# One step of a hybrid recurrent decoder layer: a recurrent head's ScalarE work cut into two visits, the residual input read in blocks and turned on VectorE, and three moved steps

## The chip, the cores and the metric

The kernel runs on 1 core of one Trainium2 chip. The metric is device time in microseconds (us) of one execution. TensorE (PE) does the matmuls, VectorE (DVE) and ScalarE (ACT) the elementwise work, GpSimd (POOL) one subtraction for every weight tile, and SyncE (SP) issues most of the loads. Each engine takes its instructions in the order of the program; engines wait for one another by semaphores.

## The reference

One layer for 544 rows: 512 tokens of a prompt and 32 of a sample group (8 sequences of 4). `x` is normalised, projected once, three recurrent branches are computed from the projection, each is multiplied by its part of `w_branch` and by a sigmoid gate, the sum goes through `w_out`, and a gated feed-forward with a short convolution follows.

```
proj = rmsnorm(x) @ w_in + b_in
lg   = log_sigmoid(ga @ w_gla_a2 + b_gla_a2) / 16              # decay of GLA, from 16 columns ga
o_gla = head_rmsnorm(gla(q, k, v, lg)) * g * silu(gg)
o_m   = head_rmsnorm(mlstm(...)) * g * sigmoid(mo)
log_a = 8 * sigmoid(xc @ w_r + b_r) * log_sigmoid(lambda)      # RG-LRU, a block of 128 channels is a "head" here
h     = scan(a = exp(log_a), sqrt(-expm1(2 log_a)) * sigmoid(xc @ w_i + b_i) * xc)
o_r   = h * gelu(ry)
x    += (sum_b sigmoid(G_b) * (o_b @ w_branch_b)) @ w_out
x    += (gelu(conv(u_a)) * conv(u_b)) @ w_down,   u = rmsnorm(x) @ w_up
y     = rmsnorm(x)
```

The outputs are `y` and the new states of all recurrences. All arrays are f32. The kernel gets close to f32 by splitting each operand into a high and a low part and making three matmul passes (high·high, high·low, low·high).

## The kernel before, in words

Activations lie with channels on partitions and the 544 rows along the free dimension. The work is a list of **units**, one for each tile of 128 output columns. A unit of `w_in`, `w_out` or `w_up` has 8 tiles of K, so 8 x 3 passes x 2 halves of 272 rows = 48 matmuls. Units 0 to 28 are the projection (0: small columns, among them `ga`; 1 to 8: q, k, v; 9 to 12: mLSTM's input; 13 to 16 and 17 to 20: RG-LRU's `rx` and `ry`; 21 to 24: `gg`; 25 to 28: `mo`). Units 29 to 52 ("gate and branch") have 48 matmuls for a gate and, after a slot in which other work may stand, 24 for the branch. 29 to 36 use GLA's output, 37 to 44 RG-LRU's, 45 to 52 mLSTM's. Units 53 to 60 are `w_out`, 61 to 104 `w_up`, then `w_down`.

A unit's weights go the same way each time: SP loads them into one of two `stage` slots (`free_stage` waits until POOL is done with the unit two before), ACT rounds them to `whi` (`hi`, L1122 and L1131; it also waits until the matmuls of the unit two before are done), POOL makes `wlo = stage - whi` (`lo`, L523), PE runs the matmuls (L602), and ACT takes the result out of PSUM (`evac`). PE may begin unit u when `lo` of u is there and `evac` of u-2 is done, so it needs `evac` of 25 for unit 27, and `evac` of 28 for unit 29.

The recurrent work runs between units. A table, filled by `plan(unit, part, steps)`, says which steps each of PE, ACT, DVE and POOL makes at each unit (part 0: after the unit; part 1: in the slot between gate and branch). All engines walk the same table, each doing its share of a step, and in the order in which the steps were planned. ACT at a unit does `hi` of u+2, `evac` of u, and then its steps.

The steps that the change and the prediction touch:

- `a2`: PE multiplies `ga` by `w_gla_a2` (L689); ACT takes two Abs out of PSUM (L1228) and goes on with Exp and Ln; DVE adds up the decays (`bc`).
- `rg` i: the gates of RG-LRU head i, 8 matmuls on PE (L808), then on ACT two Sigmoid, Tanh, Exp and Sqrt (L1329 to L1338), each kind of function with a table load of its own.
- `rgd` i: DVE's part of the same head (L1928 to L1946), with the scan L1938; L1942 ends what ACT waits for before the next head (`rg_o`), L1946 signals `or`. L1931 needs ACT's Sqrt.
- `gfin`: DVE's last step on GLA's output (L1904, L1907, L1909), which signals `og`. ACT waits for `og` before its `evac` of unit 25 (L1219).
- `rh`: PE transposes the last states of RG-LRU, in unit 31's slot; it waits for the fourth `or`.
- `sH` h, `sI` h: the state update of mLSTM for the samples. The states pass through three buffers; head 3 uses buffer 0 again, and its load waits until buffer 0 has been stored (`ch_out`).
- The residual `x`: it is loaded again as rows (`xp2`, `xs2`, after unit 48's load), and between units 53 and 54 PE turns it with 40 transposes (L591) into PSUM, from which DVE copies it to `xt` (L2126). DVE then clears `fraw` and `ssa`; SP waits for `ssa`, loads `fraw` (L463) and only then the weights of unit 57. DVE adds unit 53 to `xt` (L2136), which PE needs before unit 55.

Of the kernel before, what the change touches and what calls it, by code (L numbers as in the profile page):

```python
# [88 lines left out]
def layer(nc, io):  # L89
    ctx = ExitStack()  # L90
    with ctx:
# [270 lines left out]
        def _(sp):  # L362
# [70 lines left out]

            for n in range(3):
# [5 lines left out]
                def pair_of_units(i):  # L440
                    for r in range(2):
                        slot = (u0 + r) % 2
                        free_stage(i * 2 + (u0 + r))
                        load(slot, one(gates, i * 2 + r), KT_IN)
                        sp.dma_start(stage[:, slot, KT_IN:KT_GB], one(outs, i * 2 + r)).then_inc(s(f"branch{slot}"), 16)

                done = 0
                if n == 2:
                    done = 2
                    for i in range(done):  # L450
                        pair_of_units(i)

                    sp.wait_ge(s("om"), 1)
# [1872 lines left out]
```

## Time and profile before

| | us |
|---|---|
| median of 3 runs (lowest, highest) | 991.7 (988.83, 995.17) |
| the profiled execution | 993.07 |
| its span in the trace | 991.3 |
| busy: PE | 969.4 (98%) |
| busy: DVE, ACT, POOL | 539.4, 402.8, 310.8 |

The profile is of one execution. The span is from its first to its last instruction; the execution's own time is 1.8 us longer. A busy PE says that a matmul was in flight, not that it ran at full clock: the granted clock is a column of its own, 1.00 for 2.4 GHz and 0.50 for 1.2 GHz. With PE busy for 98% of the span, time can come or go only where PE is idle, where its clock is down, or where it does less or more.

### The profile page before, as it was taken

To read this page: it belongs to the slowest core of one execution; us is meant where nothing else is said; L and a number is where in the kernel's file an instruction comes from. 1 tells how busy PE (TensorE), PEld (TensorE's weight loads), DVE (VectorE), ACT (ScalarE), POOL (GpSimd) and SP (SyncE) were. 2 spreads that over 40 slices of the span, in tenths; PEclk is the share of its full clock that TensorE was granted. 3 is DMA by queue.
4 is the path that set the end of the run, shared out by engine and by line. 5 is a ranking of instruction groups with operands and counts; after the bars stand their busy time and mean duration, and the time that the engine had idled before them with its cause. 6 is when DMAs were issued, how large, how long until landed. Compare 5 with 4: busy or idle time off the path is not lost.

```text
span 991.3 us, 19378 instructions
## 1 busy us (share of the span) xinstructions
PE 969.4 (98%) x7550; PEld 948.7 (96%) x7550; DVE 539.4 (54%) x906; ACT 402.8 (41%) x584; POOL 310.8 (31%) x301
## 2 busy tenths in 40 slices
PE   9999999999799999899999999999999999999997
PEld 8899999898799999899999999999999999999996
DVE  5586346677725357764225467776777777312122
ACT  5632433477525555123232344444444444222122
POOL 2653433245322234333543530010000000244440
PEclk9999999999999999999999999999999999999998
DMA  5235423244122223526224422333222223533222
GB/s 149 65 86 117 108 65 81 64 111 128 47 72 64 65 64 87 159 63 209 73 65 61 103 85 85 89 94 93 85 85 85 85 85 101 122 93 88 87 59 91
DMA packets 172018, 89.62 MB, mean 90 GB/s; under 512 B 13662, under 2 KB 169956, under 8 KB 171967
## 3 DMA queue, kind: packets, MB, share of 16 engines
q1 hardware_dynamic: 154341, 79.16, 29.0%
q10 hardware_dynamic: 17626, 9.74, 3.8%
q8 instruction: 37, 0.61, 0.2%
q14 instruction: 14, 0.11, 0.0%
HBM read 82.29 MB, written 6.32 MB: 89 GB/s over the span
## 4 chain that ended last, share of the span: by engine, by line
PE 44%; issue 35%; POOL 18%; ACT 1%; DMA 1%; POOLq 0%; DVE 0%; DVEq 0%
PE ps L602 42%; POOL wlo L523 18%; PE ps L1040 1%; PE ps L591 1%; DMA xtok<-x_prompt 1%; PE ps L661 0%; ACT junk L1144 0%; PE ps L627 0%; POOLq L557 0%; PE ps L620 0%; ACT xtok L1160 0%; PE ps L1031 0%; PE ps L1032 0%; ACT whi L1122 0%; POOL blkc L513 0%
## 5 line engine op out<-in xcount | busy, mean ns | idle before, releaser
L523 POOL TENSOR_TENSOR wlo<-stage,whi 128x384 fp32r<-128x384 f32 (+3 forms) x231 | 278.3, 1232 | 428.2 <-ACT whi L1122 332.7
L602 PE MATMUL ps<-xh,whi 128*128 128x272 f32 x1536 | 322.6, 291 | 4.0 <-POOL wlo L523 3.4
L602 PE MATMUL ps<-xh,wlo 128*128 128x272 f32 x1536 | 318.6, 289 | 0.0
L602 PE MATMUL ps<-xl,whi 128*128 128x272 f32 x1536 | 317.7, 288 | 0.0
L602 PEld LDWEIGHTS ps<-xh,whi 128*128 128x128 f32 x1536 | 242.8, 189 | 9.1 <-ACT qk L1201 2.5
L602 PEld LDWEIGHTS ps<-xl,whi 128*128 128x128 f32 x1536 | 242.0, 189 | 0.0
L602 PEld LDWEIGHTS ps<-xh,wlo 128*128 128x128 f32 x1536 | 240.5, 189 | 0.0
L1122 ACT ACTIVATE whi<-stage 128x1024 fp32r<-128x1024 f32 (+3 forms) x59 | 72.1, 1222 | 148.3 <-PE ps L602 131.2
L1131 ACT ACTIVATE whi<-stage 128x1024 fp32r<-128x1024 f32 (+1 forms) x54 | 59.9, 1109 | 147.3 <-PE ps L602 142.0
L575 POOL COPY up<-fst 128x16 f32 (+1 forms) x44 | 25.7, 586 | 227.9 <-DVE ca L2182 227.1
L2182 DVE SCALAR_TENSOR_TENSOR ca<-up,par,ca 128x560 f32<-128x560 f32 x88 | 70.3, 799 | 6.1 <-DVE ca L2182 3.2
L602 PE MATMUL ps<-hh,whi 128*128 128x272 f32 x330 | 69.0, 291 | 0.0
L602 PE MATMUL ps<-hl,whi 128*128 128x272 f32 x330 | 68.2, 287 | 0.0
L602 PE MATMUL ps<-hh,wlo 128*128 128x272 f32 x330 | 68.1, 288 | 0.0
L2172 DVE TENSOR_TENSOR wlo<-stage,whi 128x1024 fp32r<-128x1024 f32 (+1 forms) x44 | 54.7, 1243 | 10.0 <-ACT whi L1131 6.0
L2222 DVE TENSOR_TENSOR yb<-xt,ps 128x544 f32<-128x544 f32 x7 | 5.0, 721 | 87.3 <-PE ps L602 87.3
L602 PEld LDWEIGHTS ps<-hl,whi 128*128 128x128 f32 x330 | 52.1, 188 | 0.0
L602 PEld LDWEIGHTS ps<-hh,whi 128*128 128x128 f32 x330 | 51.5, 188 | 0.1
L602 PEld LDWEIGHTS ps<-hh,wlo 128*128 128x128 f32 x330 | 51.6, 188 | 0.0
L1464 ACT ACTIVATE sg<-ps,par 128x544 f32<-128x544 f32 x24 | 17.1, 714 | 80.3 <-PE ps L602 74.4
L2162 DVE TENSOR_TENSOR up<-ps,rstd 128x272 f32<-128x272 f32 x44 | 19.4, 442 | 53.0 <-PE ps L602 53.0
L2106 DVE TENSOR_TENSOR sg<-sg,ps 128x544 f32<-128x544 f32 x16 | 11.5, 719 | 59.1 <-PE ps L602 56.5
(440 smaller groups left out, 1350.7 us busy)
## 6 DMA issues: line engine op xcount, KB each, us to landing
stage<-w_in SPq DMA_DIRECT2D x52, 512.0 KB, 3.9
stage<-w_up SPq DMA_DIRECT2D x44, 512.0 KB, 3.7
stage<-w_down SPq DMA_DIRECT2D x16, 704.0 KB, 4.4
stage<-w_branch SPq DMA_DIRECT2D x24, 256.0 KB, 4.2
...
```

The lines of the kernel that those rows point to most:

```text
L523: ins = pool.tensor_tensor(wlo[:, slot, a:b, 0:n], stage[:, slot, a:b, 0:n], whi[:, slot, a:b, 0:n].bitcast(F32), ALU.subtract)
L575: pool.tensor_copy(fsam(row[:, FPW:PADF])[:, :, 0:FW - 1], fs).then_inc(s("pads"), 1)
L591: return nc.tensor.transpose(out, in_, ident[0:k, 0:k])
L602: ins = mm(dst[:, r, :], w[:, slot, k0 + k, :], x(k)[:, r * HT:(r + 1) * HT], start=first and k == 0 and q == 0, stop=last and k == n - 1 ...
L1040: ins = mm(halves(1)[:, r, :], w[:, slot, k, :], x[:, KT_DOWN + k, r * HT:(r + 1) * HT], start=False, stop=k == KT_DOWN - 1 and q == 2)
L1122: func(whi[:, slot, 0:kt, 0:n], stage[:, slot, 0:kt, 0:n], ACT.Copy).then_inc(s("hi"), 1)
L1131: func(whi[:, slot, 0:kt], stage[:, slot, 0:kt], ACT.Copy).then_inc(s("hi"), 1)
L1464: func(split(sg[:]), halves(0), ACT.Sigmoid, bias=col).then_inc(s("gate_ev"), 1)
L2106: v.tensor_tensor(split(sg[:]), split(sg[:]), halves(1), ALU.mult).then_inc(s("br_mul"), 1)
L2162: v.tensor_tensor(row[:, FW - 1:FW - 1 + HT], src[:, 0, :], rstd[:, 0:HT], ALU.mult)
L2172: v.tensor_tensor(wlo[:, slot, 0:kt], stage[:, slot, 0:kt], whi[:, slot, 0:kt].bitcast(F32), ALU.subtract)\
L2182: v.scalar_tensor_tensor(out=out, in0=row[:, t:t + CONVF], scalar=par[:, bass.ds(j + (P_FW + 2 * NF * t + NF * r), 1)], in1=out, op0=ALU.m ...
```

## The change

Five parts. (1) `a2` moves into the middle of unit 1 on PE, and ACT's two Abs stand before `hi` of unit 3. (2) The residual `x` is loaded in blocks of 32 x 32 elements (36 DMAs, spread behind the loads of units 49 to 54) into `xq`, DVE turns it with 8 block transposes, and PE's 40 transposes go. (3) SP no longer waits for the stored mLSTM states before that load. (4) ACT issues the load of mLSTM head 3's state in `sI` 1 and not in `sH` 1. (5) ACT's chain of each RG-LRU head is cut: `rg` (Sigmoid, Sigmoid, Tanh) after units 23, 25, 27, 29, `rge` (Exp, Sqrt) a unit later; PE's and DVE's part of a head stand with `rg`. The diff shows, in this order, the table, SP's loads, PE (unit 1, then the transposes that go), ACT (the head's second half, `sI`, the loop over the units) and DVE.

```diff
+        for i in range(4):
+            plan(23 + 2 * i, 0, ("rg", i), ("rgd", i))
+            plan(*((24 + 2 * i, 0) if i < 3 else (30, 1)), ("rge", i))
         plan(24, 0, ("gfin", 0))
-        for i in range(3):
-            plan(24 + 2 * i, 0, ("rg", i), ("rgd", i))
-        plan(30, 1, ("rg", 3))
-        plan(30, 0, ("rgd", 3))
...
+            def tokens_in(k):
+                for a in range(4):
+                    part = io["x_prompt"][0].rearrange("(j t) (k a f) -> k a t j f", t=32, a=4, f=32)[k, a]
+                    dst = xq[32 * a:32 * a + 32, k, 0:SEQ].rearrange("p (j f) -> p j f", f=32)
+                    sp.dma_start(dst, part).then_inc(s("late_in"), 16)
+                if k < 4:
+                    part = io["x_sample"].rearrange("b t (k a f) -> a (b t) k f", a=4, f=32)[k]
+                    sp.dma_start(xq[32 * k:32 * k + 32, :, SEQ:T], part).then_inc(s("late_in"), 16)
...
-                    sp.wait_ge(s("ch_out"), 64)
-                    sp.dma_start(xp2[:], io["x_prompt"][0].rearrange("(t p) d -> p t d", p=P)).then_inc(s("late_in"), 16)
-                    sp.dma_start(xs2[:], io["x_sample"].rearrange("b t d -> (b t) d")).then_inc(s("late_in"), 16)
+            for q in range(4):
+                unit_in(2 + q // 2, q % 2)
+                tokens_in(q)
+            for q in range(2):
+                free_stage(U_OUT + q)
+                load((U_OUT + q) % 2, one(tiles(w_out, 0, KD), q), KT_IN)
+                tokens_in(4 + 2 * q)
+                tokens_in(5 + 2 * q)
...
+                if u == 1:
+                    pe.wait_ge(s("lo"), 2)
+                    gemm(halves(1), 1, 0, 4, x_of(xh), x_of(xl), last=False)
+                    v_a2(0)
+                    gemm(halves(1), 1, 4, 4, x_of(xh, 4), x_of(xl, 4), first=False).then_inc(s("gemm"), 1)
+                    continue
...
-            for j in range(KD):
-                if j >= 2:
-                    pe.wait_ge(s("xt"), j - 1)
-                for t in range(4):
-                    tr(pair(2 + j % 2)[:, t * P:(t + 1) * P], xp2[:, t, j * P:(j + 1) * P], P)
-                tr(pair(2 + j % 2)[:, SEQ:T], xs2[:, j * P:(j + 1) * P], TS).then_inc(s("xt_tr"), 1)
...
+            def v_rge(i):
                 act.wait_ge(s("rg_t"), 2 * i + 1)
                 func(rt[2][:, 0:CONVM], rt[2][:, 0:CONVM], ACT.Exp, scale=c8[:, i:i + 1]).then_inc(s("rg_t"), 1)
                 func(rt[4][:, 0:CONVM], rt[4][:, 0:CONVM], ACT.Sqrt).then_inc(s("rg_u"), 1)
...
             def v_sI(h):
                 if h == H - 1:
                     rms_of(NMC, TS)
+                if h == 1:
+                    act.wait_ge(s("ch_out"), 16)
+                    act.dma_start(ch_buf[0][:], io["state_mlstm_C"][0].rearrange("b h v k -> h v b k")[3])\
+                       .then_inc(s("ch_in3"), 16)
...
             for u in range(U_GB):
+                if u == 1:
+                    a2_abs()
                 act.wait_ge(s("gemm"), u + 1)
...
+            dve.wait_ge(s("late_in"), 576)
             for j in range(KD):
-                dve.wait_ge(s("xt_tr"), j + 1)
-                v.tensor_copy(xt[:, j, :], pair(2 + j % 2)[:, 0:T]).then_inc(s("xt"), 1)
+                v.transpose(xt[:, j, :], xq[:, j, :]).then_inc(s("xt"), 1)
+            dve.wait_ge(s("xt"), KD)
```

DVE, after the mLSTM convolution, at units 23 and 24. Before, `gfin` (`gv`, `ogh`, `ogl`) stands first and then head 0:

```order
L1904 SCALAR_TENSOR_TENSOR gv<-gv,par,gg 128x544 [waits s_t3_copied,s_evac]
L1904 SCALAR_TENSOR_TENSOR gv<-gv,par,gg 128x544 x3
L1907 CAST ogh<-gv 128x2176 [waits s_dve_step]
L1909 TENSOR_TENSOR ogl<-gv,ogh 128x2176 [waits s_stored,s_dve_step]
L1928 TENSOR_TENSOR rt_118<-rt_118,rx 128x568 [waits s_rg_copied]
L1931 SCALAR_TENSOR_TENSOR rt_119<-rt_117,rt_119 128x568 [waits s_rg_u,s_rg_t]
L1932 TENSOR_TENSOR rt_119<-rt_119,rt_118 128x568 [waits s_dve_step]
```

The same place on DVE in the changed kernel:

```order
L1942 TENSOR_TENSOR rt_117<-rt_117,rx 128x568 [waits s_rg_copied]
L1945 SCALAR_TENSOR_TENSOR rt_118<-rt_116,rt_118 128x568 [waits s_rg_u,s_rg_t]
L1946 TENSOR_TENSOR rt_118<-rt_118,rt_117 128x568 [waits s_dve_step]
...
L1960 TENSOR_TENSOR orl<-rt_119,orh 128x544 [waits s_dve_step]
L1918 SCALAR_TENSOR_TENSOR gv<-gv,par,gg 128x544 [waits s_t3_copied,s_evac]
L1918 SCALAR_TENSOR_TENSOR gv<-gv,par,gg 128x544 x3
L1921 CAST ogh<-gv 128x2176 [waits s_dve_step]
L1923 TENSOR_TENSOR ogl<-gv,ogh 128x2176 [waits s_stored,s_dve_step]
```

All of head 0 now stands ahead of `gfin`, the head's wait for ACT's Sqrt (`s_rg_u`) included.

ACT at units 24 and 25 before (the first row is `hi` of unit 26, `gg` is `evac` of 24, `mo` is `evac` of 25):

```order
L1122 ACTIVATE whi<-stage 128x1024 [waits s_gemm,s_stage0]
L1213 ACTIVATE gg<-ps,par 128x544 [waits s_gemm]
L1109 DMA s_gla_S<-ss 64x8x128 [waits s_out,s_ss_new]
L1109 DMA s_gla_S<-ss 64x8x128 x3
L1329 ACT_TABLE_LOAD [waits s_mcv]
L1329 ACTIVATE rt_117<-ps,par 128x568 [waits s_rg_mm]
...
L1338 ACTIVATE rt_119<-rt_119 128x568
L1122 ACTIVATE whi<-stage 128x1024 [waits s_gemm,s_stage1]
L1219 ACT_TABLE_LOAD [waits s_ss_new,s_og]
L1219 ACTIVATE mo<-ps,par 128x544 [waits s_gemm]
```

ACT from unit 23's steps on in the changed kernel:

```order
L1340 ACT_TABLE_LOAD [waits s_mcv]
L1340 ACTIVATE rt_116<-ps,par 128x568 [waits s_rg_mm]
L1341 ACTIVATE rt_117<-ps,par 128x568
L1346 ACTIVATE rt_118<-rt_116,sml 128x568 [waits s_c4,s_rg_copied]
L1131 ACTIVATE whi<-stage 128x1024 [waits s_gemm,s_stage0]
L1222 ACT_TABLE_LOAD
L1222 ACTIVATE gg<-ps,par 128x544 [waits s_gemm]
L1350 ACT_TABLE_LOAD
L1350 ACTIVATE rt_116<-rt_116,sml 128x568 [waits s_rg_t]
...
L1228 ACT_TABLE_LOAD [waits s_ss_new,s_og]
L1228 ACTIVATE mo<-ps,par 128x544 [waits s_gemm]
```

A head's first half now stands before `hi` of 26, its second half behind `evac` of 24; `evac` of 25 still waits for `s_og`.

DVE where the residual is turned, in the changed kernel:

```order
L2140 STREAM_TRANSPOSE xt<-xq 128x544 [waits s_late_in,s_stored]
L2140 STREAM_TRANSPOSE xt<-xq 128x544 x7
L2142 MEMSET up 128x2x2 [waits s_xt]
L2143 MEMSET fraw 128x1408
L2144 MEMSET ssa 128x544
L2151 TENSOR_TENSOR xt<-xt,ps 128x544 [waits s_gemm]
```

Before, eight copies from PSUM stood in place of the transposes, each behind five of PE's.

## Rows read from the trace of the kernel before

**Rows 1.** The page: busy us, share of the span, instructions of each engine.

```profile
PE 969.4 (98%) x7550; PEld 948.7 (96%) x7550; DVE 539.4 (54%) x906; ACT 402.8 (41%) x584; POOL 310.8 (31%) x301
```

**Rows 2.** Waits of PE: engine, line, awaited, us in total, times, longest.

```profile
PE ps L591 <- DVE orl L1946: 5.5, 1, 5.5
PE ps L602 <- POOL wlo L523: 3.8, 5, 2.0
PE ps L911 <- ACT cts L1418: 2.5, 1, 2.5
```

**Rows 3.** Windows: stretch, us, busy time of the engines, PE's granted clock, DMA.

```profile
272.00:277.00 5.00, 5.00 (x26) 4.78 (x26) 0.00 (x0) 0.59 (x1) 0.00 (x0) 0.57 0.47 133
```

**Rows 4.** Timeline of ACT, units 23 to 25: start, us, instruction, [idle before].

```profile
208.64 1.04 ACT L1122 ACTIVATE whi<-stage 128x1024 fp32r<-128x1024 f32 x1
...
212.24 1.28 ACT L1329 ACT_TABLE_LOAD   x1 [1.95 <-issue]
...
215.72 1.28 ACT L1337 ACT_TABLE_LOAD   x1
...
219.10 0.68 ACT L1338 ACTIVATE rt<-rt 128x568 f32<-128x568 f32 x1
...
222.04 0.71 ACT L1219 ACTIVATE mo<-ps,par 128x544 f32<-128x544 f32 x1
```

**Rows 5.** Timeline of DVE, `gfin` and head 0.

```profile
210.32 4.39 DVE L1904 SCALAR_TENSOR_TENSOR gv<-gv,par,gg 128x544 f32<-128x544 f32 x4 [4.97 <-ACT gg L1213]
...
216.07 2.43 DVE L1909 TENSOR_TENSOR ogl<-gv,ogh 128x2176 fp32r<-128x2176 f32 x1
...
219.89 0.75 DVE L1931 SCALAR_TENSOR_TENSOR rt<-rt,rt 128x568 f32<-128x568 f32 x1 [0.73 <-ACT rt L1338]
...
225.50 0.72 DVE L1942 TENSOR_TENSOR rt<-rt,ry 128x32 f32<-128x32 f32 x1
...
227.48 1.41 DVE L1946 TENSOR_TENSOR orl<-rt,orh 128x544 fp32r<-128x544 f32 x1
```

**Rows 6.** Timeline of PE: start of unit 27, and `rh` in unit 31.

```profile
225.10 0.49 PE L602 MATMUL ps<-xh,whi 128*128 128x272 f32 x2 [1.12 <-POOL wlo L523]
...
271.90 1.02 PE L591 MATMUL ps<-ident,rhn 128*9 128x128 f32 x4 [5.53 <-DVE orl L1946]
```

**Rows 7.** Timelines of PE and ACT around `a2`, and PE's start of unit 4.

```profile
33.26 2.10 PE L689 MATMUL ps<-ga,wa 16*128 16x272 f32 x8
35.39 1.32 ACT L1228 ACTIVATE g<-ps,par 128x544 f32<-128x544 f32 x2 [0.15 <-PE ps L689]
49.54 0.49 PE L602 MATMUL ps<-xh,whi 128*128 128x272 f32 x2 [1.96 <-POOL wlo L523]
```

**Rows 8.** Timeline of PE: the same 16 matmuls of `sI` for heads 1 and 2.

```profile
409.99 3.33 PE L911 MATMUL ps<-cts,qbm 128*32 128x129 f32 x16 [2.53 <-ACT cts L1418]
...
424.49 1.96 PE L911 MATMUL ps<-cts,qbm 128*32 128x129 f32 x16
```

**Rows 9.** Timeline of PE: its first transposes of `x`, and the starts of units 54 and 57.

```profile
529.51 0.60 PE L591 MATMUL ps<-ident,xp 128*128 128x128 f32 x4
...
535.98 0.52 PE L602 MATMUL ps<-mh,whi 128*128 128x272 f32 x2
...
554.75 0.52 PE L602 MATMUL ps<-mh,whi 128*128 128x272 f32 x2 [0.41 <-POOL wlo L523]
```

**Rows 10.** Timeline of DVE: the last `ml`, and `ssa` cleared.

```profile
526.17 1.32 DVE L2120 TENSOR_TENSOR ml<-mix,mh  x1 [0.83 <-ACT mh L1491]
...
538.36 0.51 DVE L2129 MEMSET ssa<- 128x544 f32 x1
```

**Rows 11.** Timeline of SP's `fraw` loads, and of ACT's `hi` of unit 57.

```profile
538.90 2.71 SPq L463 DMA_DIRECT2D fraw<-state_ffn_conv  x4
...
549.91 1.06 ACT L1131 ACTIVATE whi<-stage 128x1024 fp32r<-128x1024 f32 x1 [5.34 <-DMA stage<-w_out]
```

**Rows 12.** The line of DVE's block transpose: duration ns min/median/max, start, form.

```profile
L2153 DVE STREAM_TRANSPOSE fst<-fraw x1: 1630/1630/1630, 583.0 to 583.0; 128x1408 f32<-128x1408 f32 x1
```

More of the change, by code:

```diff
@@ L438, in _, with unit_in @@
                 u0 = U_GB + KD * n
-                def pair_of_units(i):
-                    for r in range(2):
[L442 to L453, printed above, removed]
-                    sp.wait_ge(s("ch_out"), 64)
-                    sp.dma_start(xp2[:], io["x_prompt"][0].rearrange("(t p) d -> p t d", p=P)).then_inc(s("late_in"), 16)
-                    sp.dma_start(xs2[:], io["x_sample"].rearrange("b t d -> (b t) d")).then_inc(s("late_in"), 16)
-                with sp.Fori(done, KD // 2) as i:
-                    pair_of_units(i)
-            load_all(U_OUT, tiles(w_out, 0, KD), 4, KT_IN)
+                def unit_in(i, r):
+                    slot = (u0 + r) % 2
+                    free_stage(i * 2 + (u0 + r))
+                    load(slot, one(gates, i * 2 + r), KT_IN)
+                    sp.dma_start(stage[:, slot, KT_IN:KT_GB], one(outs, i * 2 + r)).then_inc(s(f"branch{slot}"), 16)
+                with sp.Fori(0, KD // 2 if n < 2 else 2) as i:
+                    for r in range(2):
+                        unit_in(i, r)
+            sp.wait_ge(s("om"), 1)
+            for q in range(4):
[6 more added lines that the diff above has]
+                tokens_in(5 + 2 * q)
+            load_all(U_OUT + 2, tiles(w_out, 2 * P, KD - 2), 2, KT_IN)
             sp.wait_ge(s("ssa"), 1)
@@ L927, in nothing @@
                 pass
-            parts = {"a2": v_a2, "csn": nothing, "decays": nothing, "rgc": nothing, "rowc": nothing, "mconv": nothing, "rgd": nothing, "rows": nothing, "rowst": nothing, "smp": nothing, "rowt": v_rows, "gprep": nothing, "gA": v_gA, "gB": v_gB, "gd": v_gd, "gfin": nothing,
+            parts = {"a2": v_a2, "csn": nothing, "decays": nothing, "rgc": nothing, "rowc": nothing, "mconv": nothing, "rge": nothing, "rgd": nothing, "rows": nothing, "rowst": nothing, "smp": nothing, "rowt": v_rows, "gprep": nothing, "gA": v_gA, "gB": v_gB, "gd": v_gd, "gfin": nothing,
                      "cs": v_cs, "rg": v_rg, "rh": v_rh, "gelu": nothing, "mprep": nothing, "msilu": nothing, "mqk": v_mqk, "mA": v_mA, "mB": v_mB,
@@ L949, in _ @@
             for u in range(1, U_GB):
-                if u >= 2:
-                    pe.wait_ge(s("evac"), u - 1)
+                if u == 1:
[4 more added lines that the diff above has]
+                    continue
+                pe.wait_ge(s("evac"), u - 1)
                 unit(u, u % 2, u % 2, xh, xl)
@@ L1222, in _, with a2_abs @@
             a2v = ps[:, 2048:4096].rearrange("p (j a b) -> p j a b", j=2, a=2)[:, :, :, 0:HT]
[L1224 removed]
+            def a2_abs():
                 act.wait_ge(s("a2"), 1)
@@ L1228, in v_a2 @@
                     func(split(g1[:, j, :]), a2v[:, j], ACT.Abs, bias=par[:, P_A2 + j:P_A2 + j + 1]).then_inc(s("a2_act"), 1)
+            def v_a2(_):
                 act.wait_ge(s("a2_act"), 2)
@@ L1444, in nothing @@
                 pass
-            parts = {"a2": v_a2, "csn": nothing, "decays": v_decays, "rgc": nothing, "rowc": nothing, "mconv": nothing, "rgd": nothing, "rows": nothing, "rowst": v_rowst, "smp": nothing, "rowt": v_rows, "gprep": v_gprep, "gA": v_gA, "gB": v_gB, "gd": nothing, "gfin": v_gfin,
+            parts = {"a2": v_a2, "csn": nothing, "decays": v_decays, "rgc": nothing, "rowc": nothing, "mconv": nothing, "rge": v_rge, "rgd": nothing, "rows": nothing, "rowst": v_rowst, "smp": nothing, "rowt": v_rows, "gprep": v_gprep, "gA": v_gA, "gB": v_gB, "gd": nothing, "gfin": v_gfin,
                      "cs": v_cs, "rg": v_rg, "rh": v_rh, "gelu": v_gelu, "mprep": v_mprep, "msilu": v_msilu, "mqk": v_mqk, "mA": v_mA, "mB": v_mB,
@@ L2248, in _ @@
             output(1, 1, U_DOWN + 3)
-            dve.wait_ge(s("late_in"), 112)
+            dve.wait_ge(s("late_in"), 656)
             gained(0, 0, 0)
```

13 lines of the change are left out of this document (3 added, 10 removed).

## The prediction, made before the changed kernel was run

> **What bounds the kernel now.** I read the page's first part, then PE's waits, then windows and timelines around each wait. PE is busy 98% of the span [rows 1], so nothing is gained by a faster helper unless it ends an idle stretch of PE. There are three with a name [rows 2]: 5.5 us before `rh`, where DVE ends RG-LRU's fourth head late; 2.5 us in `sI` of mLSTM head 1, where ACT held back `cts`; and 3.8 us in five pieces before units that lacked `wlo`, of which 1.96 are before unit 4 [rows 7] and 0.41 before unit 57 [rows 9]. An idle stretch also costs behind its end. After the 5.5 us PE's granted clock averages 0.57 over 5 us [rows 3], so part of them was at 1.2 GHz instead of 2.4: 5 x 0.43 = 2.2 us lost. After the 2.5 us the same 16 matmuls took 3.33 us instead of 1.96 [rows 8]: 1.4 lost. The change also takes PE's transposes away, which occupy PE from 529.51 to 535.98, 6.5 us [rows 9]. Added up, 5.5 + 2.2 + 2.5 + 1.4 + 6.5 = 18.1 us are on offer. Whether they are got depends on what is late next.
>
> **Part 1, the heads and `og` (the largest term).** The order of the steps on DVE decides. Before, DVE does `gfin` from 210.32 to 218.50 [rows 5], while ACT goes through head 0's functions, 212.24 to 219.78 [rows 4]: side by side. Now `gfin` stands behind head 0 on DVE, and head 0 stands behind ACT's Sqrt, which is a unit later in ACT's order. ACT's `evac` of 25 waits for `og`, and PE's unit 27 for that `evac`. Step by step, in the times of the trace:
>
> - ACT ends mLSTM's last activation at about 208.7 (`hi` of 26 follows at 208.64 [rows 4]) and now starts the head there. Table load, two Sigmoid and Tanh take 215.72 - 212.24 = 3.5, to 212.2. `hi` of 26 takes 1.0, `evac` of 24 with a table load 1.3 + 0.7: 215.2. Exp and Sqrt with a load each take 219.78 - 215.72 = 4.1: 219.3.
> - DVE's head 0 from L1931 to the end of L1946 takes 228.89 - 219.89 = 9.0 [rows 5], part of it beside POOL's `lo`; I take 8.5: 227.8. `gfin` took 8.2; its cast and subtraction (1.3 + 2.4) and four operations at about 0.75 each give 6.7 as the low end. I take the low end, since POOL has nothing to do by then: `og` at 234.5, between 234 and 237.
> - ACT's table load and `mo` take 2.0 [rows 4]: 236.5. PE starts unit 27 at 236.7 instead of 225.10 [rows 6]. That is 11.6 us later, after some 13 us of idleness (it has done what is ahead of unit 27 by 223.7).
>
> The rest keeps ACT and DVE on the path. From 236.5: Sigmoid and Tanh of head 1, now without a table load, 2.2; `hi` 1.0; `evac` 0.7; Exp and Sqrt 4.1: 244.5. DVE gets from L1931 to the end of L1942 in 226.22 - 219.89 = 6.3: 250.8. ACT's first half of head 2 takes 2.2, `hi` of 30 1.5, `evac` of 28 0.7: 255.2. Unit 29 needs that `evac`; PE has been done since 250.8, so it idles 4.5 us. Exp and Sqrt follow to 259.3. PE makes unit 29 in 9.1 (72 matmuls at the 6.14 us for 48 of [rows 9], less a rounding) and head 3's matmuls in 1.8: 266.3. ACT's first half ends at 268.7, unit 30's gate at 272.4, its Sigmoid at 273.2, Exp and Sqrt at 277.3, DVE's head 3 at 277.3 + 8.1 to 9.0 = 285.4 to 286.3. PE has been waiting for it in `rh` since 281.6. So the wait that this part was to end is still there, 4 us long, and `rh` starts at about 285.8 instead of 271.90 [rows 6]: **+13.9 us**. The clock after the first idle stretch is hidden (PE waits for ACT again at unit 29); after the second it is not, and delays the gates that ACT waits for: +1.7, between the 1.4 of [rows 8] and the 2.2 of [rows 3]. After `rh` it costs what it did, or 0.5 less. Sum **+15** (12 to 18).
>
> **Part 2, `a2`.** PE's 2.0 us of `a2` [rows 7] move from behind unit 1 to its middle, so unit 1 ends 2.0 later, with up to 0.3 for the parameters that DVE is still copying. ACT's path from the end of unit 1 to unit 4's weights loses the two Abs and their wait, 0.15 + 1.35 = 1.5 [rows 7], since they are done in the idle time ahead. The rest of the path (`hi`, `evac`, Exp, Ln, `hi` of 4, `lo`) is as long as before. 2.0 + 0.2 - 1.5 = **+0.7** at unit 4, whose idle time grows from 1.96 to about 2.5. Nothing is behind it that was waiting.
>
> **Part 3, the load in `sI` 1.** ACT's `cts` copy stood behind the wait for the stored buffer. Without it the copy can follow PE's transposes of the states at once, which end three us before PE reaches `sI` at 409.99 - 2.53 = 407.46. Both the idle time and the clock loss go: 2.53 + 1.37 = **-3.9** [rows 8]. The load is issued about a microsecond later than before and needed some 20 us on.
>
> **Part 4, the residual.** PE runs unit 54 at 529.5 at once. DVE starts after the last `ml` at 527.5 [rows 10]. Its block transpose of 1408 columns took 1.63 us [rows 12]; 544 columns at the same rate are 0.63, with a fixed part 0.67, so eight are 5.4 (the low end; 6.5 if each costs 0.8 beside POOL's `lo`, which falls into this time). Clearing takes 2.2 as before, so `ssa` is clear at about 535.1 to 536.2 instead of 538.87 [rows 10]. The gain is that, not PE's 6.5: SP issues the four `fraw` loads only after `ssa` and the weights of unit 57 behind them, and those were already late [rows 11]. From `ssa` to the start of unit 57 it took 554.75 - 538.87 = 15.9 us, through these DMAs, `hi` and `lo`, and it still will, so unit 57 starts 2.7 to 3.8 us earlier, I take 3.5. PE, which has 12.9 us of work from unit 55 on in that time, idles 3 us before 57 (0.41 before), and pays a clock loss like part 3's, 1.4. Together **-2.1** (-3.8 to 0).
>
> This term rests on the blocks being there by 527.5. They are 36 loads of 32 KB and 64 KB in pieces of 128 bytes, as `fraw`'s are; SP issued four of 88 KB in 2.7 us [rows 11]. 2.1 MB at `fraw`'s rate (0.35 MB while 538.9 to about 546) are 40 us of the 60 us between the loads of units 49 and 56, beside the weights' 2 to 3 us each of six or so. It fits with some 3 us left at the end. The Trainium skill (DMA: Bandwidth & Descriptors, Specifications) says that below 512 bytes a transfer does not reach line rate; `fraw`'s rate agrees, and by that rule the last blocks are the ones at risk, which is the rival below. The waits dropped on SP (part 3 of the change's list) were over when SP came to them: no gain.
>
> **Sum.** +15.0 + 0.7 - 3.9 - 2.1 = +9.7. Against the profiled execution's 993.07 that is 1002.8; the median of the runs lies 1.4 lower, and from it the sum is 1001.4. I say 1002.
>
> **The rivals.**
> 1. *The wait for `og` does not reach PE, and the kernel gets faster.* If `og` came by 222, when PE is done with unit 26, part 1 would be -5.5 - 2.2 = -7.7 and the sum -13: 979. For it speaks that each half of a head fits into ACT's time between two units (3.5 and 4.1 of 6.1). Against it, that DVE needs 8.5 + 6.7 us after a Sqrt that ends at 219.3; the turning point is 12 us away. Between the two, a shorter `og` delay lets the later idle times shrink only one for one.
> 2. *The blocks land late.* If 128-byte pieces cost half as much again as `fraw`'s, the last ones land at about 531 to 532 and unit 55's weights behind them. DVE starts 4 us later, part 4 turns to +2: sum +14, 1006. For: six DMAs' weights share the queue, and unit 57's load behind `fraw` took 7.8 us to 549.8 where others took 3.5 to 4. Against: nothing else is on the queues there.
> 3. *The stretch in part 1 is shorter than I sum it*: PE's clock stays up, DVE without POOL beside it takes the low end each time. Part 1 is +12, part 4 the full -3.8: sum +5, 997.
> 4. *ACT's longer order loses more*: a late `hi` behind a long chain makes POOL late as well, with the 1 to 2 us that DVE's operations lose beside POOL: part 1 is +18, sum +13 to +16, up to 1008. The Trainium skill (SBUF — State Buffer, SBUF: two separate sides) says that a VectorE operation with two SBUF inputs and a GpSimd one shut each other out for a whole instruction. By it `gfin`, whose operations have two inputs, would be back at its 8.2 us if a `lo` fell into it, +1.5 for part 1; the low value that I took for it needs POOL idle.
>
> **How the numbers follow.** The main case, 0.60: 999 to 1005, likeliest 1002. Rival 1: 0.06. Rival 2: 0.10. Rival 3: 0.14. Rival 4: 0.10. For 8 in 10 the range takes the main case, rival 3 and most of rivals 2 and 4, and leaves rival 1 out: 995 to 1008. One per cent, 9.9 us, is what a measurement of this kernel can tell from no change, and 1001.6 lies in the middle of the main case: slower by over 1%: half of it and a little more (0.34), rivals 2 and 4 (0.19), together 0.53. Faster by over 1%: 0.06. Within 1%: 0.41.
>
> **What would show it.** In the profile after: PE's longest wait before unit 27, on ACT's `mo`, 11 to 15 us; ACT waiting for DVE's `ogl` there; a second of 4 to 5 us before unit 29, and still one of 3 to 5 us in `rh` on `orl`; the clock at 0.5 behind each. No wait on `cts`. Unit 4's wait at 2.4 to 2.8. No L591 on `xp`, eight STREAM_TRANSPOSE of 0.6 to 0.8 from about 13 us later in the span, DVE not waiting for a DMA before them, and a wait of 2 to 3.5 us before unit 57 on `wlo`. Wrong would be: unit 27 without a wait of over 5 us, or DVE waiting on `xq`'s loads.

## The result and the profile after

| | before | changed | ratio, 95% interval |
|---|---|---|---|
| median of 15 runs each (lowest, highest) | 990.2 (988.74, 995.17) us | 996.65 (995.59, 998.03) us | 1.0062 [1.0052, 1.0071] |
| the profiled execution: own time, span | 993.07, 991.3 us | 997.2, 995.4 us | |

The changed kernel is 6.4 us slower, 0.6%. That is inside the forecast range (995 to 1008), 5 us below its value, and within 1% of no change; the forecast had given the larger chance to over 1%.

The page of the changed kernel, first part (busy us, share, instructions):

```profile
PE 964.6 (97%) x7510; PEld 946.9 (95%) x7510; DVE 532.5 (53%) x906; ACT 404.0 (41%) x585; POOL 308.6 (31%) x301
```

PE has 40 instructions and 4.8 us of work fewer than in [rows 1], and the time is longer: what was saved in work came back as waiting. The waits of PE, to be held against [rows 2]:

```profile
PE ps L612 <- ACT mo L1228: 13.5, 2, 11.2
PE ps L612 <- POOL wlo L533: 4.1, 3, 2.4
PE ps L601 <- DVE orl L1960: 4.1, 1, 4.1
```

The wait on `cts` is gone, the one in `rh` has only shrunk from 5.5 to 4.1, and there are 13.5 us of a new kind: PE waits for ACT's `mo`, the `evac` of a unit. The timeline of PE at those places (start, us, instruction, [idle before]): units 4, 27 and 29, `rh`, the 16 matmuls of `sI` for heads 1 and 2, and unit 57.

```profile
50.15 0.49 PE L612 MATMUL ps<-xh,whi 128*128 128x272 f32 x2 [2.43 <-POOL wlo L533]
...
234.11 0.82 PE L612 MATMUL ps<-xh,whi 128*128 128x272 f32 x2 [11.22 <-ACT mo L1228]
...
253.11 0.55 PE L612 MATMUL ps<-xh,whi 128*128 128x272 f32 x2 [2.26 <-ACT mo L1228]
...
285.01 1.02 PE L601 MATMUL ps<-ident,rhn 128*9 128x128 f32 x4 [4.12 <-DVE orl L1960]
...
421.02 1.96 PE L921 MATMUL ps<-cts,qbm 128*32 128x129 f32 x16
...
434.14 1.96 PE L921 MATMUL ps<-cts,qbm 128*32 128x129 f32 x16
...
558.92 0.52 PE L612 MATMUL ps<-mh,whi 128*128 128x272 f32 x2 [1.54 <-POOL wlo L533]
```

Set each start against the same one of before, and the differences give the balance sheet of the two profiled executions. PE is done with unit 26 at 234.11 - 11.22 = 222.89, before at 225.10 - 1.12 = 223.98 [rows 6]: 1.1 us *ahead*, although unit 4 began 0.6 later [rows 7]. Unit 27 then starts 9.0 late and `rh` 13.1 late [rows 6]; PE comes to `sI` 1 13.6 late (421.02 for 409.99 - 2.53, since it no longer waits there) and to `sI` 2 9.65 late [rows 8]; unit 57 is 4.2 late [rows 9], the end of the span 4.1.

The clock explains the 1.1 us ahead. Windows of the changed kernel and, last, of before (stretch, us, busy time of PE, PEld, DVE, ACT, POOL, granted clock, DMA share, GB/s):

```profile
226.00:239.00 13.00, 4.89 (x21) 4.89 (x22) 6.67 (x7) 6.88 (x9) 1.86 (x3) 0.51 0.13 40
...
284.00:291.00 7.00, 5.99 (x27) 5.75 (x28) 1.55 (x3) 2.46 (x3) 0.00 (x0) 0.51 0.46 119
...
558.00:564.00 6.00, 5.08 (x40) 5.08 (x41) 3.67 (x4) 1.78 (x3) 3.99 (x4) 1.00 0.36 107
...
45.00:60.00 15.00, 12.57 (x101) 12.38 (x100) 13.99 (x31) 7.71 (x10) 9.82 (x9) 1.00 0.26 72
```

```profile
45.00:60.00 15.00, 13.04 (x92) 12.86 (x91) 13.00 (x30) 7.10 (x9) 8.64 (x8) 0.89 0.26 72
```

PE ran at 1.2 GHz (0.51) behind the waits before unit 27 and in `rh`, and at 2.4 GHz (1.00) behind those before units 4 and 57. Behind the wait before unit 29 it was at 1.2 GHz for 3.4 us as well, 1.7 us lost. Before, the stretch around unit 4 averaged 0.89: 15 x 0.11 = 1.7 us lost, which the changed kernel did not lose in this execution.

Where the 11.2 us come from. ACT of the changed kernel (Sqrt of head 0, then the table load and `mo` of unit 25), and DVE (head 0 from Sqrt on, its last operation, `gfin`):

```profile
217.57 0.68 ACT L1351 ACTIVATE rt<-rt 128x568 f32<-128x568 f32 x1
218.16 1.04 ACT L1131 ACTIVATE whi<-stage 128x1024 fp32r<-128x1024 f32 x1
232.05 1.28 ACT L1228 ACT_TABLE_LOAD   x1 [12.85 <-issue]
233.35 0.71 ACT L1228 ACTIVATE mo<-ps,par 128x544 f32<-128x544 f32 x1
```

```profile
218.36 0.75 DVE L1945 SCALAR_TENSOR_TENSOR rt<-rt,rt 128x568 f32<-128x568 f32 x1 [7.18 <-ACT rt L1351]
...
224.69 0.73 DVE L1960 TENSOR_TENSOR orl<-rt,orh 128x544 fp32r<-128x544 f32 x1
225.33 2.87 DVE L1918 SCALAR_TENSOR_TENSOR gv<-gv,par,gg 128x544 f32<-128x544 f32 x4
...
229.56 2.43 DVE L1923 TENSOR_TENSOR ogl<-gv,ogh 128x2176 fp32r<-128x2176 f32 x1
```

DVE sits idle for 7.18 us for ACT's Sqrt, does head 0 in 7.0 and `gfin` in 6.7, and at 232.0 gives `og`. The label `<-issue` on ACT's 12.85 us names no releaser; `ogl`'s end at 231.99 with the table load at 232.05 does.

### The profile page after: what moved, and what is told of

It is laid out like the page before. It is cut to its first block, busy times and chain, and to the rows that moved or that the text cites. A ratio compares the mean times of both kernels' runs of the same rounds, so it can differ in the third digit from the quotient of the medians.

```text
span 995.4 us, 19319 instructions
## 1 busy us (share of the span) xinstructions
PE 964.6 (97%) x7510; PEld 946.9 (95%) x7510; DVE 532.5 (53%) x906; ACT 404.0 (41%) x585; POOL 308.6 (31%) x301
## 4 chain that ended last, share of the span: by engine, by line
PE 45%; issue 35%; POOL 18%; POOLq 0%; ACT 0%; DVE 0%; DVEq 0%
PE ps L612 42%; POOL wlo L533 18%; PE ps L630 1%; PE ps L1049 1%; PE ps L601 1%; PE ps L637 0%; PE ps L671 0%; POOLq L567 0%; PE ps L1040 0%; PE ps L1041 0%; ACT whi L1131 0%; POOL blkc L523 0%; PE ps L1009 0%; POOLq L528 0%; DVE ytok L2285 0%
## 5 line engine op out<-in xcount | busy, mean ns | idle before, releaser
L612 PE MATMUL ps<-xh,whi 128*128 128x272 f32 x1536 | 323.9, 292 | 16.1 <-ACT mo L1228 13.5
```

The costliest lines, as they stand in the source:

```text
L612: ins = mm(dst[:, r, :], w[:, slot, k0 + k, :], x(k)[:, r * HT:(r + 1) * HT], start=first and k == 0 and q == 0, stop=last and k == n - 1 ...
```

## The experiments

All of them are held against runs of the kernel before on the same chip. "Ratio" is to those. The first four rows are from one chip, the next four from a second, the last four from a third. The kernel before itself spreads over 6.6 us, so a difference between two rows can come out up to 2 us apart by the medians and by the ratios (0.001 of ratio is 1 us); where that matters both are given.

| kernel | median us | ratio, 95% interval |
|---|---|---|
| gfin_first | 992.03 | 1.0007 [0.9993, 1.0021] |
| gfin_first_head3_whole | 985.69 | 0.9941 [0.9919, 0.9963] |
| heads_whole | 984.52 | 0.9923 [0.9894, 0.9952] |
| before_cut_only | 1003.12 | 1.0121 [1.0095, 1.0148] |
| two_sets | 979.09 | 0.9876 [0.9853, 0.9898] |
| heads_whole_a2_behind | 982.42 | 0.9914 [0.9898, 0.9931] |
| heads_whole_rh_late | 983.67 | 0.9936 [0.9915, 0.9956] |
| heads_whole_head3_early | 975.99 | 0.9849 [0.9829, 0.9870] |
| head3_early_a2_behind | 976.50 | 0.9857 [0.9831, 0.9883] |
| unit57_ahead_of_fraw | 974.97 | 0.9836 [0.9810, 0.9863] |
| before_load_in_sI | 988.07 | 0.9970 [0.9954, 0.9986] |
| before_residual_only | 985.76 | 0.9949 [0.9933, 0.9966] |

**gfin_first.** The theory taken from the prediction: the place of `gfin` behind head 0 makes the loss.

```diff
-        for i in range(4):
+        plan(23, 0, ("rg", 0))
+        plan(24, 0, ("gfin", 0), ("rge", 0), ("rgd", 0))
+        for i in range(1, 4):
             plan(23 + 2 * i, 0, ("rg", i), ("rgd", i))
             plan(*((24 + 2 * i, 0) if i < 3 else (30, 1)), ("rge", i))
-        plan(24, 0, ("gfin", 0))
```

> The changed kernel with one edit to the table: DVE does gfin before head 0 instead of behind it (head 0's rgd is planned at unit 24 behind gfin; ACT keeps the cut). Theory A (the order of DVE's steps): the 11.2 us before unit 27 and the 2.3 us before unit 29 exist only because og stands behind head 0. Then og is ready by about 218, unit 27 starts at about 223 without a wait, and the heads run two units apart; head 3's Exp and Sqrt still stand in unit 30's slot, so DVE ends it at about 268.5 and PE, there at 265, waits some 3 us in rh. Against the changed kernel that is -14 to -16.5 us: 980 to 983 us. Rival B (the cut itself: hi and evac between the halves make every head later on ACT, and PE waits for evac of 27 or for weights instead): PE waits 5 us or more before one of units 26 to 29 though og is early, and the time stays at 990 or more.

Measured 992.0: 4.6 below the changed kernel, not 14 to 16.5. Theory A fell, as far as it said "only"; the time is rival B's. PE's waits, then ACT at the first halves of heads 1 and 2 and the `evac` of unit 28, then the end of `gfin` on DVE:

```profile
PE ps L613 <- ACT mo L1229: 6.9, 1, 6.9
PE ps L613 <- POOL wlo L534: 6.3, 5, 2.4
PE ps L602 <- DVE orl L1961: 4.1, 1, 4.1
```

```profile
229.89 0.73 ACT L1341 ACTIVATE rt<-ps,par 128x568 f32<-128x568 f32 x1 [4.71 <-DVE rt L1957]
...
244.79 0.73 ACT L1341 ACTIVATE rt<-ps,par 128x568 f32<-128x568 f32 x1 [3.70 <-DVE rt L1957]
...
248.23 0.69 ACT L1229 ACTIVATE mo<-ps,par 128x544 f32<-128x544 f32 x1
```

```profile
220.69 2.43 DVE L1924 TENSOR_TENSOR ogl<-gv,ogh 128x2176 fp32r<-128x2176 f32 x1
```

`og` is there at 223.1 and the 11.2 us before unit 27 are gone (2.15 are left, on `wlo`), and 6.9 stand before unit 29. ACT comes to a head's first half and finds DVE not through with the head ahead (4.71 and 3.70 us), because both heads use the same temporaries. `hi` and `evac` stand behind that on ACT. So there were two mechanisms one behind the other, and the first had covered the second. The new theory (C): the cut brings the first half of head i to ACT one unit earlier, but the event that it needs, DVE's end of head i-1, comes no earlier.

**gfin_first_head3_whole.** `rge` 3 planned at (29, 0) instead of in unit 30's slot:

```diff
-            plan(*((24 + 2 * i, 0) if i < 3 else (30, 1)), ("rge", i))
+            plan(24 + 2 * i if i < 3 else 29, 0, ("rge", i))
```

> As gfin_first, and head 3's second half (Exp, Sqrt) is planned directly behind its first, after unit 29, so that head 3 is not cut. Theory A: Sqrt of head 3 ends at about 256 instead of 260.4, DVE ends the head at about 264, before PE is there (265): no wait in rh and no lower clock behind it. 3 us of waiting and 1.5 to 2 us of clock below gfin_first: 975 to 978 us. Rival B': ACT's 4 us of Exp and Sqrt ahead of unit 30's gate make that gate late and PE waits before unit 30's branch or unit 31 instead; then the time equals gfin_first's within 1 us.

The level was wrong with gfin_first's; the step was right and larger than forecast: 6.3 us below gfin_first, no wait in `rh` and no lower clock there. Of the 6.3, 4.1 are the wait. gfin_first's clock was at 0.50 for 6.8 us around `rh`, 5.6 of them behind PE's start there, so 2.8 us were lost; 0.6 comes back as waiting before unit 57. Rival B' fell.

**two_sets** tests theory C by taking away what ACT waits for.

```diff
+        rtb = [rt[0], rt[1], at("rt6", [P, PADM], rest + 4 * TB - 2304)]
+        def heads_rt(i):
+            return rt[:2] + (rtb if i % 2 else rt[2:5]) + [rt[5]]
...
-                if i:
-                    act.wait_ge(s("rg_o"), i)
+                rt = heads_rt(i)
+                if i > 1:
+                    act.wait_ge(s("rg_o"), i - 1)
```

> As gfin_first_head3_whole (985.7 us; PE waits 2.2 before unit 27, 0.9 before unit 28, 6.9 before unit 29), and heads 1 and 3 use a second set of three temporaries, so that ACT's first half of head i waits for DVE's head i-2 and no longer for head i-1. gfin_first overturned the theory that only the place of gfin counts: og came by 223 and unit 27 began at 226.8, but unit 29 still waited for mo, whose evac stands on ACT behind the first half of head 2, and that stood 3.7 us behind DVE's head 1. Theory C (the cut brings each head's first half to ACT a unit earlier, while DVE's end of the head ahead stays where it was, so ACT stands there with hi and evac behind it): without that wait ACT runs through, the 6.9 us before unit 29 fall to under 1, and with them 3.4 us of lower clock: 975 to 978 us. Rival D (the heads' work on ACT is simply too long for the time between the units, with two more table loads a head): ACT is behind even without the wait, unit 29 still waits 4 us or more: 982 to 986 us.

979.1 us, 1.1 above theory C's range, 2.9 below rival D's. PE's waits, and ACT's `hi` of unit 30:

```profile
PE ps L616 <- POOL wlo L537: 6.4, 5, 2.4
PE ps L616 <- ACT mo L1232: 2.3, 1, 2.3
```

```profile
242.75 1.48 ACT L1135 ACTIVATE whi<-stage 128x1536 fp32r<-128x1536 f32 x1 [2.37 <-PE ps L616]
```

The wait before unit 29 fell from 6.9 to 2.3, and the lower clock behind it is gone. The second set pays 6.6 us (6.4 by the ratios): C holds for most of it. The 2.3 us left (2.26, the figure of the changed kernel too) were not foreseen, and are no head's: ACT is through with its half of head 2 and stands idle for 2.37 us until PE ends unit 28. In the kernel before, PE's eight matmuls of head 2 stood between units 28 and 29 and covered ACT's `hi` and `evac` of 28 (the wait was 0.34); the new table has them before unit 28, so `hi` (1.5) and `evac` (0.7) lie open.

**heads_whole** undoes the cut in the changed kernel; **before_cut_only** makes the cut alone in the kernel before.

```diff
+        plan(24, 0, ("gfin", 0))
+        for i in range(3):
+            plan(24 + 2 * i, 0, ("rg", i), ("rge", i), ("rgd", i))
+        plan(30, 1, ("rg", 3), ("rge", 3))
+        plan(30, 0, ("rgd", 3))
```

> The changed kernel with the old table for the heads: each head in one visit on ACT, at units 24, 26, 28 and in unit 30's slot, gfin first. What is left is parts 1 to 4 of the change's list (a2, the residual, SP's wait, the load in sI 1). From the shifts between the two traces the terms are: unit 4's clock -1.3, the load -3.8, the residual -5.5, together -10.6, and the heads +14.7. Theory A: this kernel is 14.7 us below the changed one, 981.5 to 982.5 us, with unit 27 started near 224 and the wait of about 5.5 us in rh back. If the terms are not independent (rival: the waits found at sI and before unit 57 come back once PE is 13 us earlier there), it is 985 or more.

```diff
-        for i in range(3):
-            plan(24 + 2 * i, 0, ("rg", i), ("rgd", i))
-        plan(30, 1, ("rg", 3))
-        plan(30, 0, ("rgd", 3))
+        for i in range(4):
+            plan(23 + 2 * i, 0, ("rg", i), ("rgd", i))
+            plan(*((24 + 2 * i, 0) if i < 3 else (30, 1)), ("rge", i))
...
+            def v_rge(i):
```

> The kernel before with the heads' part of the change alone: the new table and the ACT chain in two visits; everything else is as before. Theory A: +14.7 us on the kernel before, less the 1 to 2 us by which the shorter stretch at unit 4 shortened the others: 1003 to 1006 us, with 11 us of waiting before unit 27, 2 to 3 before unit 29 and 4 in rh. Rival (part of the 14.7 belongs to a2's move, which shifted ACT and DVE against PE before unit 27): under 1001.

The cut costs 12.1 us on the change by the medians (996.65 - 984.52), 13.8 by the ratios (10.8 to 16.8), and 12.0 (9.4 to 14.7) on the kernel before, where 14.7 was forecast from the shifts; 1003.1 lies in theory A's range, 984.5 lies 2 above it. The waits of before_cut_only are the changed kernel's, but for 3.6 us before unit 29 instead of 2.3:

```profile
PE ps L601 <- ACT mo L1218: 14.8, 2, 11.2
PE ps L590 <- DVE orl L1947: 4.1, 1, 4.1
PE ps L910 <- ACT cts L1419: 2.8, 1, 2.8
```

That the cut makes the loss, alone and in either kernel, is shown. No wait reappears at `sI` or grows before unit 57 in heads_whole (1.3 us there), so none of the terms hid another in these traces.

**heads_whole_head3_early** and **heads_whole_rh_late** look for the gain that the cut was after, in the table of heads_whole:

```diff
-        plan(30, 1, ("rg", 3), ("rge", 3))
-        plan(30, 0, ("rgd", 3))
+        plan(29, 0, ("rg", 3), ("rge", 3), ("rgd", 3))
```

```diff
-        plan(31, 1, ("rh", 0))
-        plan(31, 0, ("mprep", 0), ("mqk", 0))
+        plan(31, 0, ("rh", 0), ("mprep", 0), ("mqk", 0))
```

> heads_whole (984.5 us) with head 3 moved whole from unit 30's slot to behind unit 29 (gfin first, heads 0 to 2 whole as before). Head 3 can start on ACT when DVE is through with head 2, at 254.6; with 6.3 us its Sqrt ends at 261 instead of 265.9, and DVE ends it at 268.5 to 269, as PE comes to rh (268.7). Against it stands that ACT's Sigmoid of gate 30 is behind the head on ACT: at 263 instead of 259.2, and PE waits some 2 us for it before unit 31. If waiting shrinks from 5.5 to 2 to 2.5 us and the clock's loss from 3.4 to 1.7: 979 to 981 us. If the gate's delay costs as much as the head gains: 984 to 986.

> heads_whole (984.5 us) with rh, the transposes of RG-LRU's last states, planned behind unit 31 instead of in its slot. PE's 3.0 us of unit 31's branch then come before the wait for DVE's head 3. If the wait in rh is a plain race between PE and the chain of head 3: 5.5 us shrink to 2.5, the stretch at the lower clock from 6.8 us to 3.4 (1.7 us less lost), and up to 0.8 comes back in front of mqk 0, which needs ACT's copy of rh: 979.5 to 981.5 us. Rival (rh's transposes are needed early by something else that then waits): over 983.

The first gained 8.5 us (7.3 by the ratios, 6.6 between the starts of units 27 and 57 in the two traces), more than the 3.5 to 5.5 that were forecast: its gate's wait before unit 31 was 0.9, not 2, and the clock stayed up. The second missed its forecast, 983.7 for 979.5 to 981.5; 0.8 below heads_whole by the medians and 1.3 above it by the ratios, it has no gain that the runs can tell. Its waits, then DVE's scan and last subtraction for head 3, and what POOL does meanwhile:

```profile
PE ps L601 <- DVE orl L1960: 3.6, 1, 3.6
...
PE ps L839 <- issue: 0.8, 1, 0.8
```

```profile
265.10 2.37 DVE L1952 TENSOR_TENSOR_SCAN rt<-rt,rt 128x568 f32<-128x568 f32 x1
...
269.77 1.76 DVE L1960 TENSOR_TENSOR orl<-rt,orh 128x544 fp32r<-128x544 f32 x1
```

```profile
263.70 4.84 POOL L533 TENSOR_TENSOR wlo<-stage,whi 128x512 fp32r<-128x512 f32 x3 [10.15 <-ACT whi L1131]
269.69 4.21 POOL L533 TENSOR_TENSOR wlo<-stage,whi 128x512 fp32r<-128x512 f32 x3 [1.15 <-ACT whi L1131]
```

PE reached `rh` later, as meant, but by going on it let ACT round and POOL subtract the next unit's weights at 269.69, and beside that DVE's `orl` took 1.76 instead of 0.72 us. Head 3 was 1 us later, and 0.8 came before `mqk`. The net is 1.2 us less waiting, and the clock did not stay up: it was at 0.50 for 6.8 us around `rh`, as in heads_whole. Of those, 5.1 fell on a busy PE here and 4.4 there, which takes 0.4 of the 1.2 back.

**before_load_in_sI** and **before_residual_only** put the other two terms on the scale, each alone in the kernel before. The edits are the change's own for those parts, cut here to a line or two of each:

```diff
             def v_sI(h):
+                if h == 1:
+                    act.wait_ge(s("ch_out"), 16)
```

```diff
-                tr(pair(2 + j % 2)[:, SEQ:T], xs2[:, j * P:(j + 1) * P], TS).then_inc(s("xt_tr"), 1)
...
-                v.tensor_copy(xt[:, j, :], pair(2 + j % 2)[:, 0:T]).then_inc(s("xt"), 1)
+                v.transpose(xt[:, j, :], xq[:, j, :]).then_inc(s("xt"), 1)
```

> The kernel before with the load of mLSTM head 3's state issued in sI 1 alone. The forecast's part 3: 2.53 of waiting and 1.37 of clock, -3.9: 986 to 987 us, no wait on cts. Rival (the load comes too late for sH 3, and a wait moves there): under 2 us of gain.

> The kernel before with the residual in blocks and DVE's transposes alone (SP's dropped wait included). The forecast's part 4 said -2.1 (-3.8 to 0), with 3 us of waiting before unit 57 and a stretch at the lower clock behind it; the shift between the two traces says -5.5, with 1.5 us of waiting and no lower clock. By the trace: 984.5 to 985.5 us; by the forecast: 988 to 989.

The load: 0.9970, -3.0 us (-4.6 to -1.4), at 988.1 a microsecond above its range. There is no wait on `cts`, and none has come behind the edit; the one wait that is new, 0.9 us on `gvt`, stands at 103 us, 300 us ahead of it. The residual: 0.9949, -5.1 us (-6.6 to -3.4), near the trace's -5.5 and not the forecast's -2.1, which lies outside. With the cut's +12.0 they make +3.9 of the +6.1 us that the change's ratio gives; the rest, +2.2 with an uncertainty larger than itself, would be `a2`'s.

**heads_whole_a2_behind** and **head3_early_a2_behind** put `a2` back: PE's part is shown, ACT's two Abs go back with it to the step behind unit 1.

```diff
-                if u == 1:
-                    pe.wait_ge(s("lo"), 2)
-                    gemm(halves(1), 1, 0, 4, x_of(xh), x_of(xl), last=False)
-                    v_a2(0)
-                    gemm(halves(1), 1, 4, 4, x_of(xh, 4), x_of(xl, 4), first=False).then_inc(s("gemm"), 1)
-                    continue
```

> heads_whole (984.5 us) with a2 back behind unit 1, as it was before the change. The profiles so far: with a2 inside unit 1 the clock was at 0.5 for 3.4 us near 33 us, just behind a2's eight matmuls of 16 rows, in three of four executions, and for 3.4 us behind unit 4's wait in two of four; each costs 1.7 us. With a2 behind unit 1: never near 33 in two, behind unit 4's wait in one of two. Theory A2 (the move costs its 0.5 us at unit 4 and, in most executions, 1.7 us of clock near 33): this is 1.5 to 2.5 us faster than heads_whole: 982 to 983 us. Rival (the move gained the 1.3 us that the one profiled execution showed): 985.5 to 986.

> heads_whole_head3_early (976.0 us) with a2 back behind unit 1: the load in sI 1 and the residual of the change, heads 0 to 2 where they were before it, head 3 whole behind unit 29. Taking a2's move back gave 2.1 us on heads_whole (984.5 to 982.4). The same here: 973.5 to 975 us, no stretch at the lower clock near 33 us. If the 2.1 was chance: 976 to 977.

The first pair gave -2.1 us (-0.9 by the ratios), the second +0.5 (+0.8), where -1 to -2.5 was expected: inconclusive, since the intervals reach 1.6 to 2.9 us to either side. The profiles tell more than the times. Windows of heads_whole, then of heads_whole_a2_behind:

```profile
30.50:37.50 7.00, 6.93 (x35) 6.34 (x36) 2.12 (x5) 1.34 (x3) 2.57 (x3) 0.76 0.31 78
50.00:57.00 7.00, 5.18 (x29) 5.21 (x30) 6.55 (x18) 4.63 (x6) 4.51 (x4) 0.76 0.44 113
```

```profile
30.50:37.50 7.00, 7.00 (x49) 6.23 (x48) 1.21 (x4) 3.74 (x6) 5.28 (x6) 1.00 0.28 75
50.00:57.00 7.00, 7.00 (x46) 7.00 (x45) 6.28 (x22) 3.00 (x4) 2.34 (x3) 0.76 0.58 152
```

A window at 0.76 over 7 us is 1.7 us lost. Of the seven profiled kernels with `a2` inside unit 1, five have it near 33 us and three near 53; of the seven with `a2` behind unit 1, none near 33 and five near 51. That is 8 and 5 losses of 1.7 in seven executions each: 1.9 and 1.2 us on average. With unit 4's 0.5 us more waiting I estimate part 2 at +1.2; its sign isn't shown by the times.

**unit57_ahead_of_fraw**, on head3_early_a2_behind:

```diff
+            free_stage(U_OUT + 4)
+            load((U_OUT + 4) % 2, one(tiles(w_out, 4 * P, KD - 4), 0), KT_IN)
...
             sp.wait_ge(s("ssa"), 1)
...
-            load_all(U_OUT + 4, tiles(w_out, 4 * P, KD - 4), KD - 4, KT_IN)
+            load_all(U_OUT + 5, tiles(w_out, 5 * P, KD - 5), KD - 5, KT_IN)
```

> As head3_early_a2_behind, and SP loads unit 57's weights before it waits for ssa and loads fraw. PE's wait before unit 57 was 1.1 to 1.5 us in the kernels with the residual in blocks, with no lower clock behind it in any profile. If SP's order sets it, the wait goes: 1.1 to 1.5 us below head3_early_a2_behind, 972.5 to 974 us. Rival (the weights queue behind the blocks of x and are late anyway, or fraw then is late for DVE): no gain, or PE waits before unit 58.

975.0 for 976.5, a microsecond above its range: PE has no wait before unit 57 any more (0.9 without the edit), and unit 58 is on time. The waiting is shown to be SP's order; the 1.5 us of time (2.1 by the ratios) are less than the intervals reach to either side (2.6). It is the fastest version run: 16 us under the kernel before, 22 under the changed one. It takes parts 2, 3 and 4 of the change's list, head 3 whole and a visit earlier, and one load moved.

## Why the prediction was right, and where it was off

| term | forecast | profiled executions | runs of single edits |
|---|---|---|---|
| part 1, heads and `og` | +15 (12 to 18) | +14.6 | +12.0 (9.4 to 14.7); +12.1, by the ratios +13.8 |
| part 2, `a2` | +0.7 | -1.1 | not resolved, estimate +1.2 |
| part 3, the load | -3.9 | -3.9 | -3.0 (-4.6 to -1.4) |
| part 4, the residual | -2.1 (-3.8 to 0) | -5.5 | -5.1 (-6.6 to -3.4) |
| sum | +9.7 | +4.1 (span) | +6.1 (the change itself, by its ratio) |

The third column is read off PE's starts: -1.1 at unit 26's end, +13.56 on coming to `sI` 1, +9.65 at `sI` 2, +4.2 at unit 57. The last column is the ratio of each single edit times 990.4, and for the second pair of part 1 the difference of the change and heads_whole. The 12 lies below the 14.6 of the two executions, but the intervals take the 14.6 in. The clock is one size in which executions differ: around `rh` it was at 0.50 for 3.4 us in before_cut_only, 3.2 of them behind PE's start there, and for 6.8 us in the changed kernel, 6.0 of them behind it: 1.6 and 3.0 us lost.

**Part 1.** The chain was forecast right in its links. Against its times: Sqrt of head 0 at 218.3 (forecast 219.3), `og` at 232.0 (234.5), unit 27 at 234.1 (236.7), a wait of 11.2 (11 to 15). A microsecond of the lead is the clock at unit 4; DVE's head 0 took 7.0 us, where 8.5 was taken from a row of before in which POOL worked beside it. `gfin` without POOL took the forecast 6.7.

The step "the clock after the first idle stretch is hidden" was right and was not followed through: between units 27 and 29 PE ran at 0.85 on average, so 105 matmuls that took 14.18 us before had 16.74. The lost clock filled the second wait from inside, 2.3 us instead of 4.5. `rh` came at 285.0; the forecast's 285.8 with its 1.7 of clock was 287.5.

What the prediction had *wrong* in part 1 is its rival 1: "if `og` came by 222, part 1 would be -7.7 and the sum -13: 979". gfin_first had `og` at 223.1 and took 992. The chain that binds next, ACT's first halves behind DVE's heads, stood in the prediction's own working as "the rest keeps ACT and DVE on the path", but the rival was priced as if it went away with `og`. Had the edit been mended by that rival, 13 us of the hoped-for gain would have been missing.

**Part 2** was priced as an idle time only: 2.43 us measured (forecast about 2.5). The price that decides, 1.7 us of clock behind that wait, was in the trace of before (0.89 in the window above) and was taken to stay; it comes in one execution and not in the next.

**Part 3** was right on the wait: there is none, and both groups of 16 matmuls take 1.96. Its second size, 1.37 us of clock, was that of one execution. Two other kernels with this wait, before_cut_only (the row below) and before_residual_only, waited 2.80 and 2.87 us, and the 16 matmuls behind took 1.96, at full clock. So the load is worth the 2.5 to 2.9 us of waiting and, in some executions, 1.4 more; its own run gave -3.0.

```profile
421.77 1.96 PE L910 MATMUL ps<-cts,qbm 128*32 128x129 f32 x16 [2.80 <-ACT cts L1419]
```

**Part 4** is the term that was mis-sized. DVE of the changed kernel, and SP's and ACT's rows to hold against [rows 10] and [rows 11]:

```profile
535.81 1.32 DVE L2134 TENSOR_TENSOR ml<-mix,mh  x1 [0.83 <-ACT mh L1505]
537.05 5.12 DVE L2140 STREAM_TRANSPOSE xt<-xq 128x544 f32<-128x544 f32 x8
...
543.84 0.51 DVE L2144 MEMSET ssa<- 128x544 f32 x1
```

```profile
544.38 2.88 SPq L473 DMA_DIRECT2D fraw<-state_ffn_conv  x4
```

```profile
554.10 1.06 ACT L1140 ACTIVATE whi<-stage 128x1024 fp32r<-128x1024 f32 x1 [4.80 <-DMA stage<-w_out]
```

From the end of the last `ml` to `ssa` cleared: 7.2 us, 11.4 before, so 4.2 gained where 3.5 was said (the eight transposes take 5.12 together). From `fraw`'s issue to `hi` of 57: 9.7 us, 11.0 before; the prediction had kept 15.9 us for the whole chain, it was 14.6. Why these loads came 1.3 us faster no run singles out. So PE idled 1.54 instead of 3 and, behind that, the clock stayed up: the 1.4 us set down for it never came in the kernels with that wait (0.6 to 1.5 us). 0.7 + 1.3 + 1.4 = 3.4 is the whole error of the term.

The rival of late blocks did not come: DVE goes from `ml` to the transposes without a wait. By the rule of the Trainium skill (DMA: Bandwidth & Descriptors, Specifications) that transfers below 512 bytes miss line rate, the last blocks were the ones at risk; SP issued them from 477 to 526 us of the changed kernel, these 49 us were enough, and the rule did not decide. The case that came nearest was rival 3 (997), in part for its own reasons: part 4 went past the -3.8 that it gave it, and DVE's head 0 took less than the 8.5 us of the sum; but the clock did fall behind unit 27's wait, which it had staying up, and part 2 was shorter too in this execution. The single edit's +12.0 for part 1 is that rival's figure as well; the intervals can't tell it from 15.

**The chances.** 0.53 for slower by over 1% rested on a centre, +9.7, that lay on the border of 9.9, so that any term mis-sized downwards decided it. Part 4's measured -5.5 was 1.7 us beyond its low end (-3.8); with it the forecast of 1002 becomes 998.6. Of the 1.9 us that are left, 1.5 are the kernel before, whose median was 991.7 over 3 runs and 990.2 over 15.
